# A two-layer MLP block on one core: squares of the down tiles added up on VectorE, the last down tile and the residual pass split into token halves

## The reference, cut to what matters

```python
for l in range(2):
    ...
    h = rms_norm(x, norm_g[l, 2]) * (1.0 + sc2) + sh2
    y = jnp.square(jax.nn.relu(h @ w_up[l])) @ w_down[l]     # 1024 -> 4096 -> 1024
    x = x + gt2 * rms_norm(y, norm_g[l, 3])
```

## Time and profile before

| | us |
|---|---|
| median of 3 runs | 2072.09 (2069.68 to 2073.25) |
| the profiled execution | 2073.55 |
| its span on the core | 2071.8 |
| TensorE busy in the span | 1949.3 (94%) |
| VectorE / ScalarE / GpSimd busy | 1171.4 / 820.6 / 138.7 |
| chain that ended last, TensorE's share | 81% |

### The profile page before, as it was taken

How to read it: one execution, slowest core, us unless ns; L and a number is a source line. 1 busy time by engine, 2 the same in 40 slices (tenths; PEclk the granted TensorE clock), 3 DMA queues, 4 the chain that set the end, 5 groups by cost and what they waited for, 6 DMA issues and landing times.

```text
span 2071.8 us, 26022 instructions
## 1 busy us (share of the span) xinstructions
PE 1949.3 (94%) x9690; PEld 1523.9 (74%) x9690; DVE 1171.4 (57%) x1870; ACT 820.6 (40%) x1376; POOL 138.7 (7%) x134
## 2 busy tenths in 40 slices
PE   7999998999899889999999999998999989999996
PEld 5777566787556667776988887776777788888775
DVE  5789668786688785665653234225555484223323
ACT  3543543343232344465543233124455563323321
POOL 0006000000101111000400000000000130000000
PEclk8999999999999999999999999999999999999998
DMA  8466035874001542111212222232111211222222
GB/s 325 179 230 243 1 118 218 302 283 180 10 6 37 191 178 87 56 62 62 82 42 102 101 90 93 81 121 82 62 62 42 82 62 61 101 102 89 94 81 81
DMA packets 46517, 232.00 MB, mean 112 GB/s; under 512 B 5112, under 2 KB 7161, under 8 KB 29402
## 3 DMA queue, kind: packets, MB, share of 16 engines
q1 hardware_dynamic: 46426, 230.78, 30.8%
HBM read 228.53 MB, written 2.10 MB: 111 GB/s over the span
## 4 chain that ended last, share of the span: by engine, by line
PE 81%; DVE 10%; ACT 3%; DMA 3%; issue 2%; POOL 1%; SPq 1%; DVEq 0%; POOLq 0%; ACTq 0%
PE banks L2146 14%; PE banks L2147 14%; PE banks L2148 14%; PE banks L2372 4%; PE banks L2477 3%; PE banks L2479 3%; PE banks L2478 3%; DVE mod_raw L1347 2%; DMA w_raw<-in_wt 2%; PE banks L2392 2%; PE banks L2298 2%; PE banks L2510 1%; PE banks L2311 1%; PE banks L2522 1%; PE banks L2536 1%
## 5 line engine op out<-in xcount | busy, mean ns | idle before, releaser
L2146 PE MATMUL banks<-h_high,w_high 128*128 128x512 f32 x904 | 359.5, 398 | 20.0 <-DVE w_low L1332 16.4
L1332 DVE TENSOR_TENSOR w_low<-w_raw,w_high 128x1024 fp32r<-128x1024 f32 x184 | 227.6, 1238 | 260.1 <-ACT w_high L546 259.9
L2147 PE MATMUL banks<-h_low,w_high 128*128 128x512 f32 x904 | 354.1, 392 | 0.0
L2148 PE MATMUL banks<-h_high,w_low 128*128 128x512 f32 x904 | 353.8, 391 | 0.0
L546 ACT ACTIVATE w_high<-w_raw 128x1024 fp32r<-128x1024 f32 x184 | 193.7, 1053 | 186.7 <-PE banks L2148 149.8
L2146 PEld LDWEIGHTS banks<-h_high,w_high 128*128 128x128 f32 x904 | 171.1, 189 | 62.0 <-DVE w_low L1332 14.7
L2146 PE MATMUL banks<-hidden_high,w_high 128*128 128x512 f32 x512 | 208.8, 408 | 0.0
L2148 PE MATMUL banks<-hidden_high,w_low 128*128 128x512 f32 x512 | 200.9, 392 | 0.0
L2147 PE MATMUL banks<-hidden_low,w_high 128*128 128x512 f32 x512 | 200.9, 392 | 0.0
L2147 PEld LDWEIGHTS banks<-h_low,w_high 128*128 128x128 f32 x904 | 171.2, 189 | 36.8 <-issue 1.9
L2148 PEld LDWEIGHTS banks<-h_high,w_low 128*128 128x128 f32 x904 | 171.1, 189 | 36.2
(11 more groups left out here) (517 smaller groups left out, 3511.9 us busy)
## 6 DMA issues: line engine op xcount, KB each, us to landing
w_raw<-in_wt SPq DMA_DIRECT2D x129, 1024.0 KB, 4.8
mod_raw<-in_wmod SPq DMA_DIRECT2D x132, 512.0 KB, 4.7
mod_first<-in_wmod SPq DMA_DIRECT2D x12, 512.0 KB, 14.2
cmp_w<-in_cmp_w SPq DMA_DIRECT2D x2, 2048.0 KB, 9.0
x<-in_xT SPq DMA_DIRECT2D x1, 2048.0 KB, 13.5
dft<-in_dft SPq DMA_DIRECT2D x1, 2048.0 KB, 13.4
out_x<-x SPq DMA_DIRECT2D x8, 256.0 KB, 2.0
hy_w<-in_hy_w SPq DMA_DIRECT2D x8, 192.0 KB, 3.3
```

What stands on the lines that cost most here:

```text
L1332: v.tensor_tensor(low[:, :, :].rearrange("p k c -> p (k c)"), RAW[b // 2][:, b % 2, :], high[:, :, :].rearrange("p k c -> p (k c)").bitcas ...
L2146: mm(out, high[:, k, :], H[:, kk, :], start=start and k == order[0], stop=False)
L2147: mm(out, high[:, k, :], L[:, kk, :], start=False, stop=False)
L2148: last = mm(out, low[:, k, :], H[:, kk, :], start=False, stop=stop and k == order[-1])
```

## The change

Only the ends of the two layers change, from the end of `up` in half 1 on.

- `down1` is no loop any more: its 16 weight tiles are written out (`n` from 0 to 13, then the last pair).
- The squares of the tiles of `Y` are added up on VectorE into `RS` (`add_down_square`, 6 additions of 128x512). TensorE multiplies by ones only at the end. The zeros, `open_squares` and `add_squares` go.
- The last pair of weight tiles (the last tile of `Y`) is done for tokens 0 to 255 first and then for 256 to 511 (`down_half`): the same weights twice, 96 matmuls of 256 tokens for 48 of 512.
- The norm and the addition to `X` are done by halves: `down_sum`, `down_root`, `down_branch`, each for "a" and "b". Those of "a" are placed beside the matmuls of "b".
- ScalarE waits for `hid1_b.3` before the first weight split of the stage.
- At the start of layer 1, the split of weight tile 2 moves into the middle of `highs` and `to_halves`, as layer 0 has it (`extra=Q`).

```diff
@@ scalar: start of a layer
-                split_high(Q, 2, "h1")
                 root("h1", 5, S, D)
-                highs("h1", NORM_T, LM[:, 0:8], Hh, S)
+                highs("h1", NORM_T, LM[:, 0:8], Hh, S, extra=Q)
@@ scalar: after up1
-                        if b % 2 and a == 1:
-                            square_tile("y2", Y[:, ds((i * 2 + b // 2) * S, S)], b // 2, b // 2, taken, 4 * q0 + 4 * i + 16 + b + 1 + PRIME)
-            root("y2", 5, S, D)
+            def down_root(h):
+                n = "ab".index(h)
+                act.wait_ge(*when(f"y2_ss_{h}.all"))
+                nc.scalar.activation(RS[:, half(n)], bank(5 + n, HS), ACT.Ln, bias=EPSC[:, :], scale=1.0 / D).then_inc(*did(f"y2_ln_{h}.all"))
+                act.wait_ge(*when(f"y2_ln_{h}.all"))
+                nc.scalar.activation(RS[:, half(n)], RS[:, half(n)], ACT.Exp, scale=-0.5).then_inc(*did(f"y2_rs_{h}.all"))
+
+            act.wait_ge(*when("hid1_b.3"))
+            for n in range(15):
+                next_tile(Q + 20 + n // 4, n % 4)
+                if n % 2:
+                    m = n // 2
+                    act.wait_ge(taken, 4 * (Q + 20) + n + 1 + PRIME)
+                    if m >= 2:
+                        act.wait_ge(*when(f"y2_acc.{max(m - 2, 1)}"))
+                    nc.scalar.activation(SQ[m % 2][:, :], Y[:, m * S:(m + 1) * S], ACT.Square).then_inc(*did(f"y2_sq.{m}"))
+            act.wait_ge(*when("y2_acc.5"))
+            act.wait_ge(*when("y2_last.a"))
+            nc.scalar.activation(SQ[1][:, half(0)], part(Y, 7, 0), ACT.Square).then_inc(*did("y2_sq_a.7"))
+            down_root("a")
+            next_tile(Q + 23, 3)
+            act.wait_ge(taken, 4 * (Q + 24) + PRIME)
+            nc.scalar.activation(SQ[1][:, half(1)], part(Y, 7, 1), ACT.Square).then_inc(*did("y2_sq_b.7"))
+            down_root("b")
@@ vector
+            def down_branch(h, ks):
+                n = "ab".index(h)
+                dve.wait_ge(*when(f"y2_rs_{h}.all"))
+                for k in ks:
+                    if k < KT:
+                        v.scalar_tensor_tensor(part(Y, k, n), part(Y, k, n), AF2[:, 24 + k:25 + k], RS[:, half(n)], mul, mul).then_inc(*did(f"y2_t_{h}.{k}"))
+                    if k:
+                        dve.wait_ge(*when(f"y2_t_{h}.{k - 1}"))
+                        v.tensor_tensor(part(X, k - 1, n), part(X, k - 1, n), part(Y, k - 1, n), add).then_inc(*did(f"y2_x.{k - 1}" if n else f"y2_x_a.{k - 1}"))
-                if a:
-                    dve.wait_ge(*when("hid1_b.3"))
-                    zero_squares("y2")
+            for n in range(15):
+                next_tile(Q + 20 + n // 4, n % 4)
+                if n % 2:
+                    m = n // 2
+                    dve.wait_ge(w_used, 4 * (Q + 20) + n + 1 + PRIME)
+                    v.tensor_tensor(Y[:, m * S:(m + 1) * S], Y[:, m * S:(m + 1) * S], bank(n % 4 - 1), add).then_inc(taken, 2)
+                    if m >= 2:
+                        add_down_square(m - 1)
+            add_down_square(6)
+            dve.wait_ge(*when("y2_mm.a"))
+            v.tensor_tensor(part(Y, 7, 0), part(Y, 7, 0), bank(2, HS), add).then_inc(*did("y2_last.a"))
+            down_branch("a", range(4))
+            dve.wait_ge(*when("y2_last.a"))
+            dve.wait_ge(w_used, 4 * (Q + 24) + PRIME)
+            v.tensor_tensor(part(Y, 7, 1), part(Y, 7, 1), bank(3, HS), add).then_inc(taken, 2)
+            down_branch("a", range(4, KT + 1))
+            dve.wait_ge(*when("y2_x_a.7"))
+            down_branch("b", range(KT + 1))
+            next_tile(Q + 23, 3)
@@ tensor
-                if a:
-                    open_squares("y2")
-                        if a and b == 0:
-                            add_squares("y2", 1, 1, "down1")
-                        if a and b == 2:
-                            add_squares("y2", 0, 0)
-            last_squares("y2", 1)
+            def down_half(h, e):
+                for k in range(KT):
+                    if h == 1 and e == 0 and k == 5:
+                        down_sum("a")
+                    kk = k + KT * e
+                    mm(bank(2 + h, HS), WH[e][:, k, :], HIDh[:, kk, half(h)], start=kk == 0, stop=False)
+                    mm(bank(2 + h, HS), WH[e][:, k, :], HIDl[:, kk, half(h)], start=False, stop=False)
+                    last = mm(bank(2 + h, HS), WL[e][:, k, :], HIDh[:, kk, half(h)], start=False, stop=kk == 2 * KT - 1)
+                return last
+            for n in range(14):
+                tile(Q + 20 + n // 4, n % 4, HIDh, HIDl, even=n % 2 == 0, hidden=1 if n < 2 else None).then_inc(w_used, 1)
+            pe.wait_ge(taken, 4 * (Q + 20) + 12 + PRIME)
+            for e in range(2):
+                pe.wait_ge(w_low, 4 * (Q + 23) + 2 + e + 1 + PRIME)
+                last = down_half(0, e)
+            last.then_inc(*did("y2_mm.a"))
+            for e in range(2):
+                down_half(1, e).then_inc(w_used, 1)
+            down_sum("b")
```

More of the change, by code:

```diff
@@ L1221, in _ @@
-            root("y2", 5, S, D)
+                if a == 0:
+                    with led.loop(act, "down0", 4) as i:
+                        for b in range(4):
+                            next_tile(i + q0 + 4, b)
+                            if b % 2:
+                                act.wait_ge(w_used, 4 * q0 + 4 * i + 16 + b + 1 + PRIME)
+                                nc.scalar.activation(Y[:, ds((i * 2 + b // 2) * S, S)], bank(b - 1), ACT.Copy).then_inc(taken, 2)
+            def down_root(h):
[4 more added lines that the diff above has]
+                nc.scalar.activation(RS[:, half(n)], RS[:, half(n)], ACT.Exp, scale=-0.5).then_inc(*did(f"y2_rs_{h}.all"))
@@ L2111, in _ @@
                         hidden(a, b, b, lambda H: H[:, ds(i * 4 + (8 - 8 * a) + b, 1), :].rearrange("p o t -> p (o t)"))
-                if a:
-                    dve.wait_ge(*when("hid1_b.3"))
-                    zero_squares("y2")
[L2115 to L2122, removed]
+                if a == 0:
+                    with led.loop(dve, "down0", 4) as i:
+                        for b in range(4):
+                            next_tile(i + q0 + 4, b)
+            for n in range(15):
[17 more added lines that the diff above has]
+            next_tile(Q + 23, 3)
     @block.tensor
@@ L2770, in _, with down_sum @@
                         tile(i + q0 + 2 - 2 * a, b, Hh, Hl).then_inc(w_used, 1)
-                if a:
-                    open_squares("y2")
-                with led.loop(pe, f"down{a}", 4) as i:
-                    for b in range(4):
-                        tile(i + q0 + 4, b, HIDh, HIDl, even=b % 2 == 0, hidden=a if b < 2 else None).then_inc(w_used, 1)
-                        if a and b == 0:
-                            add_squares("y2", 1, 1, "down1")
-                        if a and b == 2:
-                            add_squares("y2", 0, 0)
-            last_squares("y2", 1)
+                if a == 0:
+                    with led.loop(pe, "down0", 4) as i:
+                        for b in range(4):
+                            tile(i + q0 + 4, b, HIDh, HIDl, even=b % 2 == 0, hidden=0 if b < 2 else None).then_inc(w_used, 1)
+            def down_sum(h):
+                n = "ab".index(h)
+                pe.wait_ge(*when("y2_acc.6"))
+                mm(bank(5 + n, HS), ONES, RS[:, half(n)], start=True, stop=False)
+                pe.wait_ge(*when(f"y2_sq_{h}.7"))
+                mm(bank(5 + n, HS), ONES, SQ[1][:, half(n)], start=False, stop=True).then_inc(*did(f"y2_ss_{h}.all"))
+            def down_half(h, e):
[17 more added lines that the diff above has]
+            down_sum("b")
     ctx.close()
```

30 lines of the change are left out of this document (7 added, 23 removed).

## The result

The changed kernel takes 2044.65 us (median of 4 runs) beside 2071.1 for the kernel before in the same job: ratio 0.987, 95% interval 0.9846 to 0.9894. The forecast was 2042.5 (range 2038 to 2048). The four runs lie between 2039.5 and 2048.46, so the distance of 2.2 us between median and forecast says little; the trace tests the sum more closely.

A forecast was written before the change was run, and what follows sets the result against it. TensorE was taken to bound `down1`, so whatever leaves its queue returns in full. 13.8 - 0.4 us in layer 0 and 13.7 + 2.5 in layer 1 make 29.6 off 2072.09: 2042.5 us, range 2038 to 2048.

The forecast's parts named there:

- A: Head of the `down` stage: removing the zeros, the matmul with ones and what follows gains 7.45 us in each layer.
- B: Between the `down` tiles: seven matmuls with ones, 6.37 us, leave TensorE; six VectorE additions replace them at cost 0.
- C: Last pair by halves on TensorE: a new 1.15 us wait for the second weight tile; "b" ends 1.8 us later.
- the new wait costs the clock: Rival: the last pair's new wait lowers the clock, half-width matmuls run at half pace; +6.8 us, 2049.3 us; chance 0.10.
- D: VectorE behind the last pair: halves' norm and residual operations done 23.6 us after its start; split costs 1.6 us of VectorE.
- E: End of layer 1: last addition to span's end, with stores lagging 0.3 us; gain 2.5 us.
- F: End of layer 0, next layer's sums of squares: root 29.0 us after the last pair's start; loss 0.4 us.

The follow-up runs named there:

- e1: Changed kernel's written-out stage without the zeros, but squares still summed by matmuls with ones and the last pair at full width; ratio 0.9918 to the kernel before.
- e6: Changed kernel without halves (full width), the last addition of squares placed ahead of the last tile's addition on VectorE; ratio 0.9885 to the kernel before.
- e7: Changed kernel with 3 (layer 0) or 5 (layer 1) more VectorE additions in each of the first six pairs; ratio 0.9902 to the kernel before.
- e10: Kernel before, with 7 matmuls of constants in TensorE's idle time while it waits for the zeros; ratio 0.9994 to the kernel before.
- e4: Changed kernel, but ScalarE splits the last pair's second weight tile ahead of the square of the tile before; ratio 0.9854 to the kernel before.
- e5: e4 plus 8 matmuls of constants ahead of layer 1's first sums and 8 behind them; ratio 0.9849 to the kernel before.
- e2: Changed kernel without halves (full width), the last addition of squares placed behind the last tile's addition on VectorE; ratio 0.9886 to the kernel before.
- e9: e5 with only the 8 matmuls of constants ahead of the sums, none behind them; ratio 0.9865 to the kernel before.

## Why the prediction was right, and where it was off

- **A and B** hold to a tenth: from the last `up` matmul to T before took 90.19 and 90.09 us, after 76.39 and 76.43, so 13.80 and 13.66 us; predicted 13.8 and 13.7. e1 and e6 price them apart: 16.6 us (expected 16.7) and a further 12.4 (12.7). That the additions cost nothing is shown by e7; that part of A is the clock, by the trace of e10 (its ratio doesn't show it). The new wait of ScalarE on the last hidden tile costs nothing: tile 1's weights are ready 0.15 us ahead of time.
- **C.** The sequence is as forecast: second weight tile taken at T + 3.92 (4.03), sums of "a" at 8.70 (8.71) without a wait, "b" ended at 13.52 (13.55). The wait's bracket reads 0.85, since it counts from the modelled end of the matmul before; by the starts the stream is late by 1364.25 - 1363.11 - 0.12 = 1.02 us, for 1.15 predicted. The rival *the new wait costs the clock* is out: PEclk is 1.00 behind it. But the wait itself was free to avoid, as e4 shows (1.1 us in layer 1).
- **D.** VectorE starts at T + 10.72 (10.75), begins "b" at 17.53 (17.6) and ends at 23.45 (23.6). The sixteen operations of "b" take 1377.86 to 1383.80, 5.94 us, so the split costs 2 x 5.94 - 10.2 = 1.7 us, 0.11 for each extra instruction. An estimate by the formula of the Trainium skill (VectorE: DVE Perf Modes, section on the TRN2 errata) makes it 0.157 and 2.5 us, which the trace doesn't bear out. The formula does give the 0.42 us that an addition of 256 lasts, (256 + 151)/0.96 ns; but the next instruction starts before that is over (5.94/16 = 0.37 us apart).
- **E** holds: 28.87 us from T to the end before, 26.24 after, 2.6 us (2.5).
- **F is the mis-sized term.** "I put the root at T + 29.0: loss 0.4 us". It came at T + 30.0, and the loss was 32.45 to 33.82, 1.4 us. The sums began when predicted (T + 19.53); what I had wrong is how much of them falls under the low clock. By the trace's clock records the clock was low until 1402.6 before, 3.1 us into the sums; after, PEclk is 0.50 for the whole first piece of them, and the low stretch ends only at 1385.8, 5.9 us into them. At full clock (e5) the eight sums take 8.1 us; from T + 19.53 they would end at T + 27.7. So my lower bound, 27.4, was fair, a little low, and the value chosen too near it. The sum also had no term for the first body behind F, where the low clock lasts longer than before as well: 0.95 us in the first five tiles.
- The profiled execution came out 4.5 us below its forecast of 2043.95: 6.4 us of it come from the stretch ahead of the change, which scatters by 9 us over the traces; against it stand the 0.9 us that the changed stretches lack and the 1.1 us of the stretch between them. That is luck, and the median's distance of 2.2 us is partly so: I had the runs of one kernel differ by up to 2.4 us, but here they differ by 9 us in the changed kernel.

What none of the terms said is that the halves, most of the diff's lines, bring nothing in sum as they stand, by the traces (with e4's split first they bring 2.6 us, 31.6 against e6's 29.0, part of it by the shorter low clock). The prediction had both parts of it (2.5 won in E, 0.4 lost in F, each against the kernel before), but never set them against the obvious third version, full width without the matmuls with ones, which is 0.9 us shorter in each layer by itself.

**Left open.** For most runs the trace gives 1 to 5 us more than the ratio (e6: 29.0 and 24; e10: 5.6 and 1), for e1 it doesn't (16.6 and 17). Each trace is one execution, and where the clock is low in the untouched parts differs from one to the next; that this explains e10 was not shown. But all gains by trace are taken against one trace of the kernel before, with a mean granted clock of 0.971, and its 17 executions in e10's job go from 0.970 (2076.03 us) to 0.977 (2064.7 us) with a median of 0.974: it is one with much low clock, and a gain against it can be more than the typical one. Why 4.08 us of idle time ahead of the sums lowers the clock for 6.8 us in the changed kernel's traces and for 3.4 in e4's, and 4.50 us at full width for 6.8 in e6's and 3.4 in e2's, was not found either.

## What to carry to other kernels

Where TensorE is busy without a gap, price a change by what leaves its queue; small fp32 matmuls that only sum over partitions (0.91 us each here) are best replaced by additions on an engine with room, and one matmul at the end. A stall of 3 to 4 us costs more than itself, by the clock behind it (2.8 us each by e10's trace, nothing in its median): either take away what it waits for, or, where the idle time can't be avoided, try filling it with matmuls of constants (1.6 us ahead of one hand-over's sums, 0.7 to 1.8 behind them by the traces; no ratio tells it from no fill). Before splitting an end into halves, write down the plain version with the other parts of the change in it; and in a queue, put work that is ready ahead of work that waits (1.1 us by a split, 0.8 by an addition, both in layer 1).

## What the runs showed of the hardware

- Matmuls of constants in idle time kept the granted clock up in these traces: PEclk 1.00 instead of 0.50 in e10 and e5, and it fell again just where the fill was left out (e9).
- By the clock records of the changed kernel's trace, the low clock of the first body begins ahead of its first matmul, at 1392.6 with the matmul at 1394.15, 3.86 us of idle time before it; it lasts until 1399.4.
- The 0.85 us of idle time in the last pair left the clock at 1.00 in the 9.7 us behind it.
